# The last projection's first weight tile split after the last expert team's transposes, with two outputs' low weights in the second pass

## The chip, the cores and the metric

The kernel runs on one core of a Trainium2 chip. The metric is the device time of one execution in microseconds (us), the median of several runs. The core has TensorE (PE, the matrix engine, whose weight loads are listed apart as PEld), VectorE (DVE), ScalarE (ACT), GpSimd (POOL), and SyncE (SP), whose queue issues the DMA transfers. SBUF is the working memory of 128 partitions, PSUM the banks into which TensorE accumulates.

## The reference

The program is two model blocks over 256 tokens of width 1024. The first has pooling, sliding-window attention and two dense feed-forward layers; the second has a mixer, then a mixture of experts, then a gated projection, and a last norm. The change touches only the seam between the experts and the gated projection:

```python
h = h + hierarchical_moe(rms_norm_2(h, norm2_g[i]), ...)     # 32 experts, top 2
gate = jax.nn.sigmoid(rms_norm_2(h, ple_norm_g[i]) @ ple_gate_w[i])
h = h + gate * (p[i] @ ple_proj_w[i]).astype(F32)
...
return rms_norm_2(h, final_g).astype(x.dtype)
```

The matrix `ple_gate_w` (1024 x 1024, float32) is called `w_ple` in the kernel; the product with it is "the last projection". It has 8 outputs of 128 columns each, c = 0 to 7, and 8 input chunks of 128, k = 0 to 7.

## The kernel before

**Split weights.** A float32 matrix product is computed from halves of the numbers: each weight w is split into a high part (float32r, a copy by ScalarE in `split_hi`, L707 to L716) and a low part (w minus the high part, by VectorE in `split_lo`, L718 to L726). The same holds for the activations (`xh`, `xl`). A product needs three matmuls: high weights by high activations, low by high, high by low; `mm3` (L1280 to L1286) issues the three. `w_ple` comes as two transfers, each into one ring tile of 2 x 2048 columns. `halves("w_ple", i, PIECE)` names the two half tiles of transfer i, so there are four pieces of 2048 columns, each with two outputs: piece 0 holds outputs 0 and 1, piece 1 outputs 2 and 3, and so on. Piece 0 is split into the buffers `third_h` and `third_l`, piece 1 into `fourth_h` and `fourth_l`, which nothing else uses at this time; pieces 2 and 3 go to `wh` and `wl`. The semaphores `hi_done` and `lo_done` count the split pieces in order; `split_lo` waits on `hi_done` (L721), and `split_hi` of the first half waits for the transfer (L711).

**The experts.** They run as 16 teams of two experts (`for b in range(TEAMS)`, once in each engine's program). On TensorE a team is: `gate_up` (L1672, 32 matmuls), a gather of the tokens of team b + 2 (L1644, L1645; absent for the last two teams), `transposes` (L1678, 2), `combine` of the team before (L1695, 16), `down` (L1686, 16). Between them ScalarE computes `sgate` (Silu, L1140) when `gate_up` is done; VectorE computes `he` from it (L2362); the transposes wait for `he`; ScalarE copies them to `heT` (L1144), for which `down` waits; ScalarE writes `yh` from the output of `down` (L1149, two halves), VectorE writes `yl` (L2370), and `combine` waits for both. In the trace `sgate`, `he` and `heT` bear the name `work`. SP streams the weights of each team into a ring of six chunks (L520); each load waits until the chunk two teams earlier was used. Behind the last chunk it issues the two transfers of `w_ple` (L538).

**The order around the change.** Each engine runs its program strictly in order. In the last team (b = 15) ScalarE's order is: high part of piece 0 (with the wait for its transfer), `sgate`, `heT`, high part of piece 1, `yh`; then the high part of piece 2, then for each of the 8 chunks `xh` (L1153) and a square (L690), then the reciprocal root of the norm (L696, L697), the high part of piece 3, a table load and the sigmoids (L1161). VectorE's order is: low part of piece 0, `he`, low part of piece 1, `yl`; then 8 additions to the residual `hs` (L2380), 8 `xl` (L2384), the low part of piece 2, and per output the scaling by the norm (L2398), the product with the gate and the addition to `hs` (L2393, L2394), with the low part of piece 3 after output 1.

**The last projection on TensorE.** First pass: for each k, as `xh` comes, high and low weights of outputs 0 to 3 by `xh` (64 matmuls, L1792). Then the squares of the norm are summed (L1276). Second pass: for outputs 0 to 3, high weights by `xl` (32 matmuls, L1798), after each output a release `ple_psum`. Then outputs 4 to 7 with `mm3` (24 matmuls each, L1285), with sums of the last norm's squares after each. These squares are computed by GpSimd (L678) as the chunks of `hs` come; GpSimd also adds pairs of the projection norm's squares (L578).

Of the kernel before, what the change touches and what calls it, by code (L numbers as in the profile page):

```python
# [16 lines left out]
KD = D // P  # L17
N_META = 16
SEQ = 256
# [24 lines left out]
TEAMS = NE // TEAM  # L44
# [3 lines left out]
CHUNKS = 3  # L48
# [5 lines left out]
PIECE = 2048  # L54
# [13 lines left out]
FIRST_PIECE = {_name: NUMBER[_name, 0] for _name, _ in SPLIT}  # L68
# [72 lines left out]
def bass_two_blocks(nc, a, out):  # L141
# [4 lines left out]
    with ctx:  # L146
# [5 lines left out]
        def sem(name):  # L152
            if name not in sems:
                sems[name] = ctx.enter_context(nc.semaphore(name))
            return sems[name]
# [37 lines left out]
        with ExitStack() as turn:  # L193
            xh = sb("xh", [P, 9, SEQ], F32R, turn)
            xl = sb("xl", [P, 9, SEQ], F32R, turn)
# [28 lines left out]
        ps = ctx.enter_context(nc.psum_tensor("ps", [P, 8, 512], F32))  # L224
# [149 lines left out]
        for part in SPLIT:  # L374
            if part in THIRD:
                k = 2
            elif part in FOURTH:
                k = 3
            else:
                k, turn_of = turn_of, 1 - turn_of  # L380
# [326 lines left out]
        def split_hi(act, name, slot, rnd, i, j, size):  # L707

            if j == 0:
                act.wait_ge(sem(f"tile_ready{slot}"), loaded(name, slot, rnd))  # L710

            buffer_free(act, name, i, j)
            high, _ = split_buffer(name, i, j)
            for to, src in parts_of(name, high, ring[:, slot, j * size:(j + 1) * size], size):
                ins = act.activation(to, src, ACT.Copy)  # L715
            ins.then_inc(sem("hi_done"), 1)  # L716

        def split_lo(dve, name, slot, rnd, i, j, size):  # L718

            piece = NUMBER[name, i * 2 + j] if type(i) is int else i * 2 + (FIRST_PIECE[name] + j)  # L720
            dve.wait_ge(sem("hi_done"), piece + 1)  # L721
            high, low = split_buffer(name, i, j)
            w = ring[:, slot, j * size:(j + 1) * size]
            for (to, src), (h, _) in zip(parts_of(name, low, w, size), parts_of(name, high, w, size)):
                ins = dve.tensor_tensor(to, src, h.bitcast(F32), ALU.subtract)  # L725
            ins.then_inc(sem("lo_done"), 1)  # L726
# [13 lines left out]
        PLE_BANK = (4, 5, 7, 0, 1, 2, 3, 4)  # L740
# [4 lines left out]
        def halves(name, i, size):  # L745
            slot, rnd = tile_at(FIRST[name] + i)
            return [(slot, rnd, i, j, size) for j in range(2)]
# [105 lines left out]
        def _(act):  # L853
# [279 lines left out]
            act.wait_ge(sem("route_ready"), 1)  # L1133
            for b in range(TEAMS):
                extra(b)
                if b == TEAMS - 1:
                    act.wait_ge(sem("chunk_used"), b * CHUNKS)
                    split_hi(act, "w_ple", *halves("w_ple", 0, PIECE)[0])
                act.wait_ge(sem("chunk_used"), b * CHUNKS + GU_CHUNKS)
                act.activation(sgate, ps[:, 4, 0:FE], ACT.Silu).then_inc(sem("sg_ready"), 1)  # L1140
                if b + 2 < TEAMS:
                    gathered(b + 2)
                act.wait_ge(sem("het_psum"), b + 1)
                act.activation(heT.rearrange("p c n -> p (c n)"), ps[:, 4, 0:FE], ACT.Copy).then_inc(sem("heT_ready"), 1)  # L1144
                if b == TEAMS - 1:
                    split_hi(act, "w_ple", *halves("w_ple", 0, PIECE)[1])
                act.wait_ge(sem("chunk_used"), (b + 1) * CHUNKS)
                for i in range(2):
                    act.activation(yh[:, i * 512:(i + 1) * 512], ps[:, 6 + i, :], ACT.Copy).then_inc(sem("y_ready"), 1)  # L1149
# [106 lines left out]
        def _(pe):  # L1256
            mm = pe.matmul
# [41 lines left out]
            for c in range(KD):  # L1299
# [4 lines left out]
                for k in range(2):  # L1304
                    ins = mm(ps[:, c % 4, 0:T], pw[:, g, k, c % 2 * P:c % 2 * P + P], pooled[:, 2 * g + k, :],
                             start=(k == 0), stop=(k == 1))
# [473 lines left out]
            def ple_weights(c, k):  # L1780
                at = slice(k * 256 + c % 2 * P, k * 256 + c % 2 * P + P)
                return [x[:, at] for x in split_buffer("w_ple", c // 4, c // 2 % 2)]

            for k in range(KD):
                pe.wait_ge(sem("xh_ready"), 4 * KD + k + 1)
                for c in range(4):
                    if k == 0 and c % 2 == 0:
                        pe.wait_ge(sem("lo_done"), FIRST_PIECE["w_ple"] + c // 2 + 1)
                    if k == 0 and c == 3:
                        pe.wait_ge(sem("hs_odd"), 5 * (KD // 2) + 1)  # L1790
                    for part, w in enumerate(ple_weights(c, k)):
                        mm(ps[:, PLE_BANK[c], 0:SEQ], w, xh[:, k, 0:SEQ], start=(k == 0 and part == 0), stop=False)  # L1792
            for q in range(KD):
                sum_squares("ple", q, SEQ)
            for c in range(4):
                for k in range(KD):
                    pe.wait_ge(sem("x_ready"), 4 * KD + k + 1)
                    ins = mm(ps[:, PLE_BANK[c], 0:SEQ], ple_weights(c, k)[0], xl[:, k, 0:SEQ], start=False, stop=(k == KD - 1))  # L1798
                ins.then_inc(sem("ple_psum"), 1)
            for c in range(4, KD):  # L1800
                pe.wait_ge(sem("lo_done"), FIRST_PIECE["w_ple"] + c // 2 + 1)
# [185 lines left out]
        def _(dve):  # L1987
# [368 lines left out]
            placed(0)  # L2356
            for b in range(TEAMS):
                extra(b)
                if b == TEAMS - 1:
                    split_lo(dve, "w_ple", *halves("w_ple", 0, PIECE)[0])  # L2360
                dve.wait_ge(sem("sg_ready"), b + 1)
                dve.scalar_tensor_tensor(he, ps[:, 4, FE:2 * FE], small[:, 178:179], sgate, ALU.mult, ALU.mult)\  # L2362
                   .then_inc(sem("he_ready"), 1)
                if b + 2 < TEAMS:
                    gathered(b + 2)
                if b == TEAMS - 1:
                    split_lo(dve, "w_ple", *halves("w_ple", 0, PIECE)[1])
                for i in range(2):
                    dve.wait_ge(sem("y_ready"), 2 * b + i + 1)
                    dve.tensor_tensor(yl[:, i * 512:(i + 1) * 512], ps[:, 6 + i, :], yh[:, i * 512:(i + 1) * 512].bitcast(F32),  # L2370
                                      ALU.subtract).then_inc(sem("y_low"), 1)
                if b + 1 < TEAMS:
                    dve.wait_ge(sem("he_ready"), b + 1)
                    placed(b + 1)
                if b % 2 and b + 3 < TEAMS:
                    selected(b // 2 + 2)
# [5 lines left out]
            for c in range(KD):  # L2382
                dve.wait_ge(sem("xh_ready"), 4 * KD + c + 1)
                dve.scalar_tensor_tensor(xl[:, c, :], hs[:, c, N_META:], V("ple", c), xh[:, c, :].bitcast(F32),  # L2384
                                         ALU.mult, ALU.subtract).then_inc(sem("x_ready"), 1)
            split_lo(dve, "w_ple", *halves("w_ple", 1, PIECE)[0])
            dve.wait_ge(sem("r_ready"), NORM["ple"] + 1)
            dve.wait_ge(sem("pp_ready"), KD)
# [162 lines left out]
```

## Time and profile before

| | |
|---|---|
| device time, 3 runs | 1058.27 us median (1054.91 to 1059.91) |
| the profiled execution | 1055.95 us, its span 1054.2 us |
| TensorE busy | 975.9 us (93%) |
| VectorE busy | 540.5 us (51%) |
| ScalarE busy | 414.4 us (39%) |
| GpSimd busy | 146.2 us (14%) |
| granted TensorE clock, mean | 0.962 of full speed |

The two experts' lines L1672 and L1686 and the last projection stand in the last quarter of the span: the experts end at about 1011 us, the projection and the last norm fill the rest. Times in the views are microseconds from the start of the span. A row of a timeline gives start, busy time, engine, line, operation and operands, and in brackets how long the engine sat idle before it and what released it. The granted clock (PEclk) has two levels here, 1.00 (2.4 GHz) and 0.50 (1.2 GHz); a value between them is a mean over a stretch with both.

### The profile page before, as it was taken

To read this page: it belongs to the slowest core of one execution; us is meant where nothing else is said; L and a number is where in the kernel's file an instruction comes from. 1 tells how busy PE (TensorE), PEld (TensorE's weight loads), DVE (VectorE), ACT (ScalarE), POOL (GpSimd) and SP (SyncE) were. 2 spreads that over 40 slices of the span, in tenths; PEclk is the share of its full clock that TensorE was granted. 3 is DMA by queue.
4 is the path that set the end of the run, shared out by engine and by line. 5 is a ranking of instruction groups with operands and counts; after the bars stand their busy time and mean duration, and the time that the engine had idled before them with its cause. 6 is when DMAs were issued, how large, how long until landed. Compare 5 with 4: busy or idle time off the path is not lost.

```text
span 1054.2 us, 16922 instructions
## 1 busy us (share of the span) xinstructions
PE 975.9 (93%) x6840; PEld 813.6 (77%) x6840; DVE 540.5 (51%) x1002; ACT 414.4 (39%) x690; POOL 146.2 (14%) x207
## 2 busy tenths in 40 slices
PE   4699999999989999999998999879889999999796
PEld 2599999998868899999987999659745555455285
DVE  4654554437874655554445548574623344333355
ACT  4443334437565634334444457633211111111152
POOL 5323233110000233322000000000100000000002
PEclk7899999999989999999999999769899999999989
DMA  7325553468721345534552512028369999999801
GB/s 294 149 91 180 197 195 109 166 192 214 184 81 35 127 170 200 188 109 172 198 200 87 203 76 85 7 84 330 160 229 417 420 421 418 419 419 420 355 1 40
DMA packets 36798, 212.01 MB, mean 201 GB/s; under 512 B 2528, under 2 KB 16112, under 8 KB 17520
## 3 DMA queue, kind: packets, MB, share of 16 engines
q1 hardware_dynamic: 36720, 210.91, 53.1%
q8 instruction: 56, 0.92, 0.4%
q14 instruction: 22, 0.18, 0.1%
HBM read 209.83 MB, written 1.07 MB: 200 GB/s over the span
## 4 chain that ended last, share of the span: by engine, by line
PE 81%; DVE 9%; ACT 3%; DMA 2%; issue 2%; POOL 2%; POOLq 0%; DVEq 0%; ACTq 0%
PE ps L1285 48%; PE ps L1672 9%; PE ps L1686 5%; PE ps L1695 3%; PE ps L1276 3%; DMA ring<-in_w_ple 2%; PE ps L1209 2%; PE ps L1644 2%; PE ps L1645 1%; DVE mix L1819 1%; DVE wl L725 1%; DVE third_l L725 1%; PE ps L1792 1%; DVE hs L571 1%; PE ps L1217 1%
## 5 line engine op out<-in xcount | busy, mean ns | idle before, releaser
L725 DVE TENSOR_TENSOR wl<-ring,wh 128x2048 fp32r<-128x2048 f32 (+3 forms) x104 | 205.2, 1976 | 189.4 <-ACT wh L715 189.4
L715 ACT ACTIVATE wh<-ring 128x2048 fp32r<-128x2048 f32 (+3 forms) x104 | 172.4, 1660 | 266.7 <-PE ps L1285 264.8
L1285 PE MATMUL ps<-xh,wh 128*128 128x256 f32 (+3 forms) x600 | 171.2, 285 | 0.0
L1285 PE MATMUL ps<-xl,wh 128*128 128x256 f32 (+3 forms) x600 | 169.4, 282 | 0.0
L1285 PE MATMUL ps<-xh,wl 128*128 128x256 f32 (+3 forms) x600 | 169.4, 282 | 0.0
L1285 PEld LDWEIGHTS ps<-xh,wh 128*128 128x128 f32 (+3 forms) x600 | 111.0, 185 | 1.2 <-issue 0.9
L1285 PEld LDWEIGHTS ps<-xh,wl 128*128 128x128 f32 (+3 forms) x600 | 111.0, 185 | 0.2
L1285 PEld LDWEIGHTS ps<-xl,wh 128*128 128x128 f32 (+3 forms) x600 | 110.9, 185 | 0.0
L1285 PE MATMUL ps<-acth,wh 128*128 128x272 f32 (+1 forms) x352 | 101.1, 287 | 0.0
L1285 PE MATMUL ps<-actl,wh 128*128 128x272 f32 (+1 forms) x352 | 100.0, 284 | 0.0
L1285 PE MATMUL ps<-acth,wl 128*128 128x272 f32 (+1 forms) x352 | 100.0, 284 | 0.0
L1285 PE MATMUL ps<-xhT,wl 128*128 128x272 f32 x320 | 92.6, 289 | 0.0
L1285 PE MATMUL ps<-xlT,wh 128*128 128x272 f32 x320 | 92.2, 288 | 0.0
L1285 PE MATMUL ps<-xhT,wh 128*128 128x272 f32 x320 | 91.3, 285 | 0.0
L1285 PEld LDWEIGHTS ps<-acth,wh 128*128 128x128 f32 x352 | 66.5, 189 | 0.2
L1285 PEld LDWEIGHTS ps<-acth,wl 128*128 128x128 f32 x352 | 66.1, 188 | 0.2
L1285 PEld LDWEIGHTS ps<-actl,wh 128*128 128x128 f32 x352 | 66.2, 188 | 0.0
L2370 DVE TENSOR_TENSOR yl<-ps,yh 128x512 fp32r<-128x512 f32 x32 | 20.6, 685 | 87.6 <-ACT yh L1149 87.6
L1285 PEld LDWEIGHTS ps<-xhT,wh 128*128 128x128 f32 x320 | 60.4, 189 | 0.0
L1285 PEld LDWEIGHTS ps<-xlT,wh 128*128 128x128 f32 x320 | 60.1, 188 | 0.0
L1285 PEld LDWEIGHTS ps<-xhT,wl 128*128 128x128 f32 x320 | 60.1, 188 | 0.0
L1686 PE MATMUL ps<-wring,work 128*64 128x512 f32 x256 | 58.5, 598 | 0.6 <-ACT work L1144 0.6
(418 smaller groups left out, 1853.1 us busy)
## 6 DMA issues: line engine op xcount, KB each, us to landing
wring<-in_w_eg SPq DMA_DIRECT2D x32, 2048.0 KB, 15.0
ring<-in_w_gu SPq DMA_DIRECT2D x22, 2048.0 KB, 8.1
wring<-in_w_ed SPq DMA_DIRECT2D x16, 2048.0 KB, 13.5
ring<-in_w_dn SPq DMA_DIRECT2D x16, 1408.0 KB, 5.9
ring<-in_w_z SPq DMA_DIRECT2D x7, 2048.0 KB, 7.8
ring<-in_w_out SPq DMA_DIRECT2D x4, 1152.0 KB, 5.1
ring<-in_w_q SPq DMA_DIRECT2D x8, 512.0 KB, 6.3
ring<-in_w_o SPq DMA_DIRECT2D x8, 512.0 KB, 17.0
```

The costliest lines, as they stand in the source:

```text
L571: eng.tensor_tensor(hs[:, c, cols], hs[:, c, cols], mix[:, c, 0:n], ALU.add).then_inc(hs_add(c), 1)
L715: ins = act.activation(to, src, ACT.Copy)
L725: ins = dve.tensor_tensor(to, src, h.bitcast(F32), ALU.subtract)
L1209: pe.matmul(ps[:, 2 * j + g, 0:n], w[:, k * 256 + g * P:k * 256 + g * P + P], xa[:, k, 0:n], start=(k == 0 and part == 0), stop=False)
L1217: ins = pe.matmul(ps[:, 2 * j + g, 0:n], w[:, k * 256 + g * P:k * 256 + g * P + P], xb[:, k, 0:n], start=False, stop=(k == KD - 1))
L1276: mm(ps[:, 6, 0:n], ones[0:rows, :], square_at(name, c + 1 - chunks)[0:rows, 0:n], start=(c < chunks), stop=(c == last))\
L1285: ins = mm(o, p, q, start=first and n == 0, stop=last and n == 2)
L1644: mm(out, h2h[:, k, at], select[:, k, :], start=(k == 0), stop=False)
L1672: ins = mm(ps[rows, 4, :], x[:, k, rows], chunk(b, c)[:, j, i * 512:(i + 1) * 512], start=(k == 0), stop=(k == KD - 1))
L1686: ins = mm(ps[rows, 6 + i, :], heT[:, k, rows], chunk(b, GU_CHUNKS)[:, j, k * D + i * 512:k * D + (i + 1) * 512], start=(k == 0), stop=(k ...
L1695: ins = mm(ps[:, c // 2, c % 2 * SEQ:(c % 2 + 1) * SEQ], y[:, c * P:(c + 1) * P], weights, start=False, stop=last and y is parts[-1], skip ...
L2370: dve.tensor_tensor(yl[:, i * 512:(i + 1) * 512], ps[:, 6 + i, :], yh[:, i * 512:(i + 1) * 512].bitcast(F32), ALU.subtract).then_inc(sem(" ...
```

## The change

In the last team, ScalarE no longer makes the high part of piece 0 ahead of `sgate`: it makes those of pieces 0 and 1 one after the other, behind `heT` and ahead of `yh`. VectorE makes the low part of piece 0 behind `he` (where that of piece 1 was), and that of piece 1 behind the eight `xl`, ahead of the low part of piece 2. On TensorE the first pass uses both parts of the weights for outputs 0 and 1 but the high part alone for outputs 2 and 3 (48 matmuls); their 16 matmuls of low weights by `xh` go to the second pass. The waits change with them: for the low part of piece 0 and the high part of piece 1 ahead of the first pass, for the low part of piece 1 ahead of output 2 of the second pass. No transfer moves and no operation is added or taken away.

```diff
--- before.py
+++ after.py
@@ -1133,9 +1133,6 @@
             act.wait_ge(sem("route_ready"), 1)
             for b in range(TEAMS):
                 extra(b)
-                if b == TEAMS - 1:
-                    act.wait_ge(sem("chunk_used"), b * CHUNKS)
-                    split_hi(act, "w_ple", *halves("w_ple", 0, PIECE)[0])
                 act.wait_ge(sem("chunk_used"), b * CHUNKS + GU_CHUNKS)
                 act.activation(sgate, ps[:, 4, 0:FE], ACT.Silu).then_inc(sem("sg_ready"), 1)
                 if b + 2 < TEAMS:
@@ -1143,7 +1140,8 @@
                 act.wait_ge(sem("het_psum"), b + 1)
                 act.activation(heT.rearrange("p c n -> p (c n)"), ps[:, 4, 0:FE], ACT.Copy).then_inc(sem("heT_ready"), 1)
                 if b == TEAMS - 1:
-                    split_hi(act, "w_ple", *halves("w_ple", 0, PIECE)[1])
+                    for x in halves("w_ple", 0, PIECE):
+                        split_hi(act, "w_ple", *x)
                 act.wait_ge(sem("chunk_used"), (b + 1) * CHUNKS)
                 for i in range(2):
                     act.activation(yh[:, i * 512:(i + 1) * 512], ps[:, 6 + i, :], ACT.Copy).then_inc(sem("y_ready"), 1)
@@ -1781,21 +1779,26 @@
                 at = slice(k * 256 + c % 2 * P, k * 256 + c % 2 * P + P)
                 return [x[:, at] for x in split_buffer("w_ple", c // 4, c // 2 % 2)]
 
+            pe.wait_ge(sem("lo_done"), FIRST_PIECE["w_ple"] + 1)
+            pe.wait_ge(sem("hi_done"), FIRST_PIECE["w_ple"] + 2)
             for k in range(KD):
                 pe.wait_ge(sem("xh_ready"), 4 * KD + k + 1)
                 for c in range(4):
-                    if k == 0 and c % 2 == 0:
-                        pe.wait_ge(sem("lo_done"), FIRST_PIECE["w_ple"] + c // 2 + 1)
                     if k == 0 and c == 3:
                         pe.wait_ge(sem("hs_odd"), 5 * (KD // 2) + 1)
-                    for part, w in enumerate(ple_weights(c, k)):
+                    for part, w in enumerate(ple_weights(c, k)[0:2 - c // 2]):
                         mm(ps[:, PLE_BANK[c], 0:SEQ], w, xh[:, k, 0:SEQ], start=(k == 0 and part == 0), stop=False)
             for q in range(KD):
                 sum_squares("ple", q, SEQ)
             for c in range(4):
+                if c == 2:
+                    pe.wait_ge(sem("lo_done"), FIRST_PIECE["w_ple"] + 2)
                 for k in range(KD):
                     pe.wait_ge(sem("x_ready"), 4 * KD + k + 1)
-                    ins = mm(ps[:, PLE_BANK[c], 0:SEQ], ple_weights(c, k)[0], xl[:, k, 0:SEQ], start=False, stop=(k == KD - 1))
+                    high, low = ple_weights(c, k)
+                    if c >= 2:
+                        mm(ps[:, PLE_BANK[c], 0:SEQ], low, xh[:, k, 0:SEQ], start=False, stop=False)
+                    ins = mm(ps[:, PLE_BANK[c], 0:SEQ], high, xl[:, k, 0:SEQ], start=False, stop=(k == KD - 1))
                 ins.then_inc(sem("ple_psum"), 1)
             for c in range(4, KD):
                 pe.wait_ge(sem("lo_done"), FIRST_PIECE["w_ple"] + c // 2 + 1)
@@ -2356,15 +2359,13 @@
             placed(0)
             for b in range(TEAMS):
                 extra(b)
-                if b == TEAMS - 1:
-                    split_lo(dve, "w_ple", *halves("w_ple", 0, PIECE)[0])
                 dve.wait_ge(sem("sg_ready"), b + 1)
                 dve.scalar_tensor_tensor(he, ps[:, 4, FE:2 * FE], small[:, 178:179], sgate, ALU.mult, ALU.mult)\
                    .then_inc(sem("he_ready"), 1)
                 if b + 2 < TEAMS:
                     gathered(b + 2)
                 if b == TEAMS - 1:
-                    split_lo(dve, "w_ple", *halves("w_ple", 0, PIECE)[1])
+                    split_lo(dve, "w_ple", *halves("w_ple", 0, PIECE)[0])
                 for i in range(2):
                     dve.wait_ge(sem("y_ready"), 2 * b + i + 1)
                     dve.tensor_tensor(yl[:, i * 512:(i + 1) * 512], ps[:, 6 + i, :], yh[:, i * 512:(i + 1) * 512].bitcast(F32),
@@ -2383,6 +2384,7 @@
                 dve.wait_ge(sem("xh_ready"), 4 * KD + c + 1)
                 dve.scalar_tensor_tensor(xl[:, c, :], hs[:, c, N_META:], V("ple", c), xh[:, c, :].bitcast(F32),
                                          ALU.mult, ALU.subtract).then_inc(sem("x_ready"), 1)
+            split_lo(dve, "w_ple", *halves("w_ple", 0, PIECE)[1])
             split_lo(dve, "w_ple", *halves("w_ple", 1, PIECE)[0])
             dve.wait_ge(sem("r_ready"), NORM["ple"] + 1)
             dve.wait_ge(sem("pp_ready"), KD)
```

## Rows read from the trace of the kernel before

**Rows 1.** Chain of work that ended last: start us, us, what ran.
```profile
969.32 1.91 PE ps L1695 x16
...
978.29 18.37 DMA ring<-in_w_ple
...
996.73 1.92 ACT third_h L715
...
998.74 2.29 DVE third_l L725
```

**Rows 2.** Timeline of TensorE: start, busy us, instruction, idle before and its releaser.
```profile
974.64 7.04 PE L1672 MATMUL ps<-wring,work 128*64 128x512 f32 x32
982.75 0.44 PE L1678 MATMUL ps<-cst,work 128*128 128x128 f32 x2 [1.07 <-DVE work L2362]
...
985.02 3.65 PE L1686 MATMUL ps<-wring,work 128*64 128x512 f32 x16
988.50 7.04 PE L1672 MATMUL ps<-wring,work 128*64 128x512 f32 x32
1001.48 0.69 PE L1678 MATMUL ps<-cst,work 128*128 128x128 f32 x2 [5.94 <-DVE work L2362]
...
1003.04 0.41 PE L1695 MATMUL ps<-places,yl 128*128 128x256 f32 x1
1003.25 0.41 PE L1695 MATMUL ps<-places,yh 128*128 128x256 f32 x1
...
1005.31 3.65 PE L1686 MATMUL ps<-wring,work 128*64 128x512 f32 x16
1011.03 0.36 PE L1695 MATMUL ps<-places,yh 128*128 128x256 f32 x1 [2.06 <-ACT yh L1149]
```

**Rows 3.** Timeline of ScalarE (ACT), same columns.
```profile
981.73 0.38 ACT L1140 ACTIVATE work<-ps 128x256 f32<-128x256 f32 x1 [5.78 <-PE ps L1672]
983.22 0.39 ACT L1144 ACTIVATE work<-ps 128x256 f32<-128x256 f32 x1 [1.11 <-PE ps L1678]
...
1017.60 0.40 ACT L690 ACTIVATE mix<-hs 128x256 f32<-128x256 f32 x1
...
1025.20 1.90 ACT L715 ACTIVATE wh<-ring 128x2048 fp32r<-128x2048 f32 x1
```

**Rows 4.** Timeline of VectorE (DVE), same columns.
```profile
982.21 0.48 DVE L2362 SCALAR_TENSOR_TENSOR work<-ps,small,work 128x256 f32<-128x256 f32 x1 [2.19 <-ACT work L1140]
...
1014.85 4.30 DVE L2384 SCALAR_TENSOR_TENSOR xl<-hs,vec,xh 128x256 fp32r<-128x256 f32 x8
1019.07 2.28 DVE L725 TENSOR_TENSOR wl<-ring,wh 128x2048 fp32r<-128x2048 f32 x1
1025.51 0.42 DVE L2398 TENSOR_TENSOR mix<-ps,rstd 128x256 f32<-128x256 f32 x1 [4.16 <-PE ps L1798]
```

**Rows 5.** Stretches: length; PE, PEld, DVE, ACT, POOL busy; PEclk, DMA share, GB/s.
```profile
1001.50:1003.50 2.00, 2.00 (x10) 2.00 (x11) 0.00 (x0) 1.29 (x2) 0.00 (x0) 0.50 0.03 8
1011.70:1015.00 3.30, 3.30 (x18) 3.30 (x17) 3.02 (x9) 2.96 (x9) 0.74 (x1) 0.52 0.00 0
```

**Rows 6.** Timeline of TensorE, last projection.
```profile
1022.11 2.32 PE L1276 MATMUL ps<-mix,ones 128*128 128x256 f32 x10
1024.08 2.25 PE L1798 MATMUL ps<-xl,third_h 128*128 128x256 f32 x16
...
1030.79 0.28 PE L1285 MATMUL ps<-xl,wh 128*128 128x256 f32 x1
1032.57 0.67 PE L1276 MATMUL ps<-sq,ones 128*128 128x256 f32 x2 [1.50 <-POOL sq L678]
```

**Rows 7.** Timeline of GpSimd (POOL), squares of the last two norms.
```profile
1016.66 1.01 POOL L578 TENSOR_TENSOR mix<-mix 128x256 f32<-128x256 f32 x1 [0.66 <-ACT mix L690]
1029.83 2.59 POOL L678 TENSOR_TENSOR sq<-hs 128x256 f32<-128x256 f32 x1 [12.16 <-DVE hs L2394]
1033.24 0.61 POOL L678 TENSOR_TENSOR sq<-hs 128x256 f32<-128x256 f32 x1 [0.82 <-DVE hs L2394]
```

## Prediction

> **What bounds the kernel now.** I read the page first: TensorE is busy 93% of the span, so only its idle time and its time at the lower clock are to be had. Then the chain of waits near the end, where the change is. In it the reader should see that TensorE's chain is broken behind the last team's `gate_up`: a transfer of `w_ple`, issued at 978.29 us, takes 18.37 us, and behind it stand the high part of piece 0 (1.92), and its low part (2.29) [rows 1]; `he` (0.48) [rows 4] follows on the same engine. So the last team's transposes wait for a weight that they don't need, only because ScalarE and VectorE work in program order.
>
> The timeline of TensorE gives the size. Team 14 is the model of an undisturbed last team, since neither it nor team 15 gathers: its `gate_up` ends at 974.64 + 7.04 = 981.68 and its transposes start at 982.75, 1.07 us later. Team 15's `gate_up` ends at 988.50 + 7.04 = 995.54, and its transposes start at 1001.48 behind 5.94 us of idleness [rows 2]. The rest of the sum is read from the views behind that: the clock by stretch, the last projection on TensorE, and the other engines' timelines.
>
> **The change, part by part.** Everything up to 995.54 stays, the transfers included: SP waits for the same `chunk_used` counts, which team 14 gives.
>
> *Step 1, the stall.* `sgate` now starts when `gate_up` is done, as in team 14 (981.73), and `he` at once behind it (982.21) [rows 3, 4]. The transposes start at 995.54 + 1.07 = 996.61 in place of 1001.48: **4.87 us** won.
>
> *Step 2, the clock.* Behind the 5.94 us the granted clock is 0.50 [rows 5], the 1.2 GHz level. There the matmuls of `combine` follow one another at 1003.25 - 1003.04 = 0.21 us [rows 2]; at full clock the same 16 took 1.91 us [rows 1], 0.119 each. Team 14's 1.07 us of idleness was followed by no such fall: from its transposes to the end of `down` are 985.02 + 3.65 - 982.75 = 5.92 us, against 1005.31 + 3.65 - 1001.48 = 7.48 in team 15 [rows 2]. I take 5.92: **1.56 us** won, `down` ends at 1002.53 in place of 1008.96. The bounds are 0 (the fall comes anyway) and 1.56.
>
> *Step 3, the copies ahead of `yh`.* `heT` starts 0.47 us behind the transposes and lasts 0.39 [rows 2, 3], so it ends at 997.47. The transfer landed by 996.73 [rows 1] and is no longer waited for. The two high parts, some 1.9 us each [rows 1, 3], end at about 1001.3; `yh` is due at 1002.5. This cover is 1.2 us: `yh` waits only if the transfer lands after about 998.7, and then us for us. VectorE's low part of piece 0 (2.29) runs from 999.4 to 1001.7, and `yl` is due at about 1003.2. So both cost nothing, and the idleness behind `down` stays at the 2.06 us shown [rows 2]: `combine` starts at 1011.03 - 6.43 = 1004.60. Queued behind the two copies on ScalarE are `yh`, the high part of piece 2 and the eight `xh`; all move up by the same 6.43.
>
> *Step 4, the first pass.* It loses 16 matmuls of 1.91 / 16 = 0.119 us [rows 1], so 1.91 us, and the norm's sums start at 1022.11 - 6.43 - 1.91 = 1013.77. What would be late instead: `xh` and the squares. The last square ended at 1018.00 [rows 3], GpSimd's last pair sum at 1017.67 [rows 7]; with the 6.43 both are at about 1011.5, so they don't hold TensorE. The new waits ahead of the pass (low part of piece 0, high part of piece 1) were met by 1001.7. Cost nothing.
>
> *Step 5, the second pass.* It gains the same 16 matmuls, so TensorE's total work is unchanged, and from output 4 on the shift is 6.43 again. It starts at 1024.08 - 8.34 = 1015.74 and comes to output 2 behind 16 matmuls, at about 1017.7. VectorE ends `xl` at 1019.15 - 6.43 = 1012.7, and then makes the low part of piece 1 (2.3) until 1015.0 and that of piece 2 (2.3) until 1017.3 [rows 4]. The first is due at 1017.7 (cover 2.7), the second at output 4, about 1021.6. Behind them on VectorE is the scaling of output 0, which was due at 1025.51 - 8.34 = 1017.17 [rows 4], when VectorE is just free. Should it be late by the whole 2.28 us, ScalarE's high part of piece 3 (1.90) and a table load stand ahead of the first sigmoid and hide most of it.
>
> *Step 6, the idle time after output 4.* Output 4 ended at 1030.79 + 0.28 = 1031.07 and TensorE then sat 1.50 us for GpSimd's first square of `hs` [rows 6], 2.59 us long, where the next took 0.61 [rows 7]. That square hangs on the norm, which comes 8.34 us earlier (step 4), while output 4 comes only 6.43 earlier. It is done at 1032.42 - 8.34 = 1024.08, against 1031.07 - 6.43 = 1024.64: the **1.50 us** go, with 0.56 us to spare. Bounds 0 and 1.50. From there TensorE's work binds, output by output, to the end as before.
>
> The long square ran while VectorE made the low part of piece 3. The Trainium skill (SBUF — State Buffer, on the shared port pair) says that a GpSimd operation that reads SBUF and a VectorE one with two SBUF inputs lock each other out for a whole instruction. The trace agrees with its 2.59 beside 0.61. It speaks against moving a low part, of that very kind, to a place where GpSimd works; here GpSimd's pair sums are over by then, and by the rule the sum stays the same.
>
> *The sum:* 4.87 + 1.56 + 1.50 = **7.93 us**. Against the profiled execution's own time that is 1055.95 - 7.93 = 1048.0. The median of the runs shown is 2.3 us above that execution: 1058.27 - 7.93 = 1050.3. If what made the other runs longer is a later transfer, the new kernel doesn't feel it (step 3); if it is something else, it does. I take the middle, 1049.2.
>
> **The rivals.**
> *A: the second fall of the clock goes too.* Behind the 2.06 us of idleness the clock was 0.52 from 1011.7 to 1015.0 [rows 5]. From 1011.03 to 1022.11 lie 16 + 64 matmuls, 11.08 us, against 80 x 0.119 = 9.55: the fall costs 1.53. It followed a stretch that had already been slow once; with TensorE fuller ahead of it, it may stay away. Against: the idle time is as long as before. Gain 9.46, time 1047.7 by the same middle. The Trainium skill (TensorE: Matmul & The Clock Gate, Part 1) says that where the transition falls varies from run to run of one kernel. That leaves both cases open.
>
> *B: a cover fails.* GpSimd's 0.56 us is the thinnest: a second lock-out, or VectorE late at 1017.2, brings back up to 1.50. Or the clock falls already behind the 1.07 us (1.56 back). Gain 4.87 to 6.4, time about 1051.5.
>
> *C: the stall isn't there in most runs.* It depends on 1.1 us between `gate_up`'s end and the landing. If transfers ran ahead by 3 us or more in the other runs, piece 0's parts would be nearly done by 995.5 and only steps 4 to 6 would count: gain 1.5 to 3, time about 1056. Against: the other runs are mostly longer, not shorter, than the profiled one.
>
> *D: slower.* The clock falls behind the 2.06 us and stays at 1.2 GHz, since TensorE's work now meets more waits. A matmul of the projection then costs 0.21 in place of 0.119 [rows 1, 2]. The gain is eaten after 7.93 / 0.091 = 87 more such matmuls; if the level stayed down through the projection, about 190 matmuls beyond those already slow, it would cost 17 and end at about 1066. Against: both falls shown ended while TensorE was working.
>
> **How the numbers follow.** Forecast (7.93) 0.50, A 0.22, B 0.17, C 0.08, D 0.03. The range holds the forecast, A and B over the spread of the runs shown: from 1054.91 - 9.46 = 1045.5 to 1059.91 - 6.43 = 1053.5. A difference under 0.5% (5.3 us) is about what a measurement of this kernel can't tell from no change. Faster by more: forecast, A and two thirds of B, 0.84; within: the rest of B and C, 0.13; slower: D, 0.03.
>
> **What would show it.** Step 1: `sgate` starts 0.05 us behind `gate_up`, and the idle time before the last transposes is about 1.1 us, with no transfer in the chain. Step 2: the last `combine` but one takes 1.9 us. Step 3: ScalarE is idle before `yh`, and TensorE's idleness before the last `combine` is still 2.06. Step 5: no idle time before output 2 of the second pass. Step 6: none after output 4. The prediction is wrong if `yh` waits behind the copies, if the clock is low for longer than the one stretch of 3.3 us that rows 5 show, or if TensorE waits for GpSimd or VectorE in the last projection.

## The result

The changed kernel takes 1048.05 us (median of 5 runs, 1046.90 to 1050.14) against 1058.22 for the kernel before in the same comparison (1054.18 to 1059.91). The ratio is 0.9915, with a 95% interval of 0.9896 to 0.9933: some 9 us less, between 7 and 11. The profiled execution took 1047.29 us, its span 1045.5.

Spans of two executions differ by what happened hundreds of microseconds earlier, too. So from here on one measure is used for all traces, **M: the time from the end of the last team's `gate_up` to the end of the span**, since all that the change touches lies in it. Before, M is 1054.2 - 995.54 = 58.66 us [rows 2]; after, 1045.5 - 996.46 = 49.04. That is 9.62 less, while the spans differ by 8.7: `gate_up` ended 0.92 later in the execution of after.

The chain of waits of the changed kernel around the last transposes (start us, us, what ran; in the new file `gate_up` is L1670, `sgate` L1137, `he` L2363, `transposes` L1676):

```profile
989.59 6.89 PE ps L1670 x32
...
996.50 0.39 ACT work L1137
...
996.99 0.49 DVE work L2363
...
997.53 0.44 PE ps L1676 x2
...
1003.51 0.03 ACT yh L1147
```

The reader should see what is gone against [rows 1]: no transfer and no split stands between `gate_up` and the transposes, only `sgate` and `he`. The timeline of TensorE gives the sizes:

```profile
989.42 7.04 PE L1670 MATMUL ps<-wring,work 128*64 128x512 f32 x32
997.53 0.44 PE L1676 MATMUL ps<-cst,work 128*128 128x128 f32 x2 [1.07 <-DVE work L2363]
...
999.81 3.65 PE L1684 MATMUL ps<-wring,work 128*64 128x512 f32 x16
1005.53 0.36 PE L1693 MATMUL ps<-places,yh 128*128 128x256 f32 x1 [2.07 <-ACT yh L1147]
```

The idle time before the last transposes is 1.07 us in place of 5.94 [rows 2]; from the transposes to the end of `down` are 999.81 + 3.65 - 997.53 = 5.93 us in place of 7.48. The idle time before the last `combine` is unchanged, 2.07. ScalarE and VectorE of the changed kernel, to be held against [rows 3, 4]:

```profile
996.50 0.38 ACT L1137 ACTIVATE work<-ps 128x256 f32<-128x256 f32 x1 [5.78 <-PE ps L1670]
...
998.28 1.90 ACT L715 ACTIVATE third_h<-ring 128x2048 fp32r<-128x2048 f32 x1
1000.08 1.90 ACT L715 ACTIVATE fourth_h<-ring 128x2048 fp32r<-128x2048 f32 x1
1003.51 1.08 ACT L1147 ACTIVATE yh<-ps 128x512 fp32r<-128x512 f32 x2 [1.53 <-PE ps L1684]
```

```profile
1000.22 2.29 DVE L725 TENSOR_TENSOR third_l<-ring,third_h 128x2048 fp32r<-128x2048 f32 x1 [2.75 <-ACT third_h L715]
...
1008.94 4.24 DVE L2385 SCALAR_TENSOR_TENSOR xl<-hs,vec,xh 128x256 fp32r<-128x256 f32 x8
1013.09 2.28 DVE L725 TENSOR_TENSOR fourth_l<-ring,fourth_h 128x2048 fp32r<-128x2048 f32 x1
1015.29 2.28 DVE L725 TENSOR_TENSOR wl<-ring,wh 128x2048 fp32r<-128x2048 f32 x1
1017.50 0.74 DVE L2400 TENSOR_TENSOR mix<-ps,rstd 128x256 f32<-128x256 f32 x2
```

Both high parts end at 1001.98, and ScalarE then sits idle for 1.53 us before `yh`: the copies are hidden. The low part of piece 1 (`fourth_l`) ends at 1015.37, and output 2 of the second pass starts on TensorE at 1017.26, with no idle time before it. The scaling of output 0 starts at 1017.50, right when the low part of piece 2 is done. TensorE around the sums of the norm and after output 4, and GpSimd's squares, which answer to [rows 6, 7]:

```profile
1013.21 2.32 PE L1274 MATMUL ps<-mix,ones 128*128 128x256 f32 x10
1015.18 2.25 PE L1801 MATMUL ps<-xl,third_h 128*128 128x256 f32 x16
...
1023.79 0.28 PE L1283 MATMUL ps<-xl,wh 128*128 128x256 f32 x1
1023.91 0.59 PE L1274 MATMUL ps<-sq,ones 128*128 128x256 f32 x2
```

```profile
1020.94 2.59 POOL L678 TENSOR_TENSOR sq<-hs 128x256 f32<-128x256 f32 x1 [8.84 <-DVE hs L2396]
1024.35 0.62 POOL L678 TENSOR_TENSOR sq<-hs 128x256 f32<-128x256 f32 x1 [0.82 <-DVE hs L2396]
```

No idle time stands in front of the sum at 1023.91, where [rows 6] have 1.50. GpSimd's first square is still 2.59 us long, but it ends at 1023.53, 0.54 us ahead of output 4 (1023.79 + 0.28).

The clock by stretch (length; busy time of PE, PEld, DVE, ACT, POOL; granted clock, DMA share, GB/s):

```profile
996.50:1002.00 5.50, 4.47 (x28) 2.92 (x30) 2.27 (x2) 4.36 (x4) 0.00 (x0) 1.00 0.29 118
1005.50:1008.00 2.50, 2.47 (x21) 2.50 (x22) 1.72 (x6) 2.16 (x5) 0.00 (x0) 1.00 0.00 0
```

The granted clock is 1.00 (2.4 GHz) in both stretches where [rows 5] show 0.50 and 0.52. So neither fall came here, and the forecast had the second one.

### The profile page after: what moved, and what is told of

Read it like the earlier page. It is cut to its first block, busy times and chain, and to the rows that moved or that the text cites. A ratio compares the mean times of both kernels' runs of the same rounds, so it can differ in the third digit from the quotient of the medians.

```text
span 1045.5 us, 16918 instructions
## 1 busy us (share of the span) xinstructions
PE 973.9 (93%) x6835; PEld 809.7 (77%) x6840; DVE 540.0 (52%) x1002; ACT 414.2 (40%) x690; POOL 146.6 (14%) x207
## 3 DMA queue, kind: packets, MB, share of 16 engines
HBM read 209.83 MB, written 1.07 MB: 202 GB/s over the span
## 4 chain that ended last, share of the span: by engine, by line
PE 83%; DVE 9%; ACT 3%; issue 2%; POOL 2%; DMA 0%; POOLq 0%; DVEq 0%; ACTq 0%
PE ps L1283 48%; PE ps L1670 11%; PE ps L1684 5%; PE ps L1693 3%; PE ps L1274 3%; PE ps L1642 2%; PE ps L1207 2%; PE ps L1643 2%; DVE mix L1822 1%; DVE wl L725 1%; PE ps L1215 1%; DVE hs L571 1%; PE ps L1628 1%; DVE third_l L725 1%; PE ps L1790 1%
## 5 line engine op out<-in xcount | busy, mean ns | idle before, releaser
L1670 PE MATMUL ps<-wring,xb_even 128*64 128x512 f32 x256 | 58.5, 607 | 2.2 <-issue 2.2
```

The source lines that it names most:

```text
L1670: ins = mm(ps[rows, 4, :], x[:, k, rows], chunk(b, c)[:, j, i * 512:(i + 1) * 512], start=(k == 0), stop=(k == KD - 1))
```

## The experiments

All measures in one place. "Idle 1" and "idle 2" are TensorE's idle times before the last transposes and before the last `combine`; T is the time from these transposes to the end of `down`; "sq" is the idle time after output 4. A fall is a stretch at 0.50. The traces of e3, i1 and i2 stand with those runs.

| kernel | M | idle 1 | T | idle 2 | sq | fall behind idle 1 | behind idle 2 |
|---|---|---|---|---|---|---|---|
| before | 58.66 | 5.94 | 7.48 | 2.06 | 1.50 | yes | yes |
| after | 49.04 | 1.07 | 5.93 | 2.07 | 0 | no | no |
| after, once more | 50.60 | 1.07 | 5.93 | 2.07 | 0 | no | yes |
| e1, splits only | 52.63 | 1.07 | 5.93 | 2.55 | 1.43 | no | yes |
| e2, second pass only | 56.67 | 6.20 | 8.37 | 2.07 | 0 | yes | no |
| e4, before, low part 3 later | 57.37 | 6.14 | 8.36 | 2.07 | 0 (0.56 later) | yes | no |
| e5, before, transfer late | 58.21 | 5.99 | 8.43 | 2.07 | 1.49 | yes | no |
| e6, after, transfer late | 49.08 | 1.08 | 5.92 | 2.07 | 0 | no | no |
| e7, before, transfer later | 61.64 | 9.43 | 8.44 | 2.07 | 1.49 | yes | no |
| e8, after, transfer later | 51.87 | 1.07 | 5.93 | 3.17 | 0 | no | yes |
| e9, before, stall filled | 55.32 | 5.64, filled | 5.94 | 2.07 | 1.49 | no | no |

**Each part alone (e1, e2).** The first experiment keeps TensorE's program and moves only the splits; both low parts are then ahead of `yl`. The second undoes just that move in the changed kernel.

```diff
 e1, against before; ScalarE (VectorE likewise, with split_lo, behind he):
-                if b == TEAMS - 1:
-                    act.wait_ge(sem("chunk_used"), b * CHUNKS)
-                    split_hi(act, "w_ple", *halves("w_ple", 0, PIECE)[0])
...
                 if b == TEAMS - 1:
-                    split_hi(act, "w_ple", *halves("w_ple", 0, PIECE)[1])
+                    for x in halves("w_ple", 0, PIECE):
+                        split_hi(act, "w_ple", *x)
 e2, against after: high and low part of piece 0 again ahead of sgate and he
```

> Before, with the splits of pieces 0 and 1 moved behind heT on ScalarE and behind he on VectorE, both low parts still ahead of yl, TensorE's program untouched. Measure: from the end of the last team's gate_up to the end of the span, 58.7 us in the kernel before, 49.0 after. Theory (the stall and its clock carry the gain, 4.87 + 1.56): idle time before the last transposes 1.1 us; yl about 0.6 us later, since VectorE now makes two low parts ahead of it; the 1.5 us before GpSimd's square stay. That gives 52.8, or 51.3 if the second fall of the clock is gone too. Rival (the second pass carries the gain): above 57.

> After, with piece 0 split ahead of sgate and he again, as before; the low weights of outputs 2 and 3 stay in the second pass. Theory: the 5.94 us of idleness before the last transposes stay, the wait for GpSimd's first square after output 4 goes: 58.7 - 1.5 = 57.2 us from the end of gate_up to the end. Rival (the second pass carries the gain): 53 or less.

e1 measured 52.63 us, against 52.8 expected with a fall; its ratio to the kernel before is 0.9929 (0.9905 to 0.9953). e2 measured 56.67 against 57.2; its ratio is 0.9992 (0.9980 to 1.0005). By these ratios the moved splits carry 7.5 of some 9 us, and the second pass alone can't be told from no change; the traces give it the 1.5 us of the column sq and little more. In e1's timelines the second pass's own use is to be seen (TensorE, then VectorE):

```profile
997.34 0.44 PE L1676 MATMUL ps<-cst,work 128*128 128x128 f32 x2 [1.07 <-DVE work L2358]
...
1005.82 0.55 PE L1693 MATMUL ps<-places,yh 128*128 128x256 f32 x1 [2.55 <-issue]
```

```profile
1000.03 2.29 DVE L725 TENSOR_TENSOR third_l<-ring,third_h 128x2048 fp32r<-128x2048 f32 x1 [2.75 <-ACT third_h L715]
1002.24 2.29 DVE L725 TENSOR_TENSOR fourth_l<-ring,fourth_h 128x2048 fp32r<-128x2048 f32 x1
1004.44 1.28 DVE L2367 TENSOR_TENSOR yl<-ps,yh 128x512 fp32r<-128x512 f32 x2
```

The low part of piece 1 stands between `third_l` and `yl` there, so `yl` starts at 1004.44, and idle 2 is 2.55 in place of 2.07. Moving 16 matmuls into the second pass lets that low part go behind `xl`: it is worth 0.5 us there, and lets the 1.43 us before GpSimd's square go. The rest of the 3.59 us between e1 and the changed kernel is the fall behind the 2.55 us.

**The transfer moved (e5 to e8).** The same one-line edit to the kernel before and to the changed one; the wait of SP ahead of the first transfer of `w_ple`:

```diff
-            for i, count in ((0, (TEAMS - 2) * CHUNKS + 1), (1, (TEAMS - 1) * CHUNKS)):
+            for i, count in ((0, (TEAMS - 1) * CHUNKS), (1, (TEAMS - 1) * CHUNKS)):           # e5, e6
+            for i, count in ((0, (TEAMS - 1) * CHUNKS + 1), (1, (TEAMS - 1) * CHUNKS + 1)):   # e7, e8
```

> Before, with the first transfer of w_ple issued only when team 14 has used its last chunk (some 10 us later, together with the second). Theory: the stall is the landing of this transfer, so the idle time before the last transposes grows from 5.9 us by as much as the transfer lands later, about 2 to 4 us, and the time from gate_up to the end grows by the same, 60.7 to 62.7. Rival (the stall is the two splits alone): 58.7.

> After, with the same late transfer. Theory (step 3's cover): the idle time before the last transposes stays at 1.07; yh waits for the two high parts only by what the landing is later than 2.2 us behind the end of gate_up. Landing 3 us behind: both high parts end at 6.8 and yh, due at 7.05, doesn't wait, 49.0 us. Landing 5 us behind: yh waits 1.8 us, about 50.9 us and perhaps a fall of the clock (1.5 more). Rival (the change only moves the wait): as much longer as the kernel before becomes.

These two missed their aim. In e5 the transfer was issued 10 us later and landed 1.24 us behind `gate_up`, where the earlier one of the kernel before had landed 1.19 us behind: issued behind a full queue it had taken 18.4 us [rows 1], and issued behind a shorter one 8.0. The DMA rates bear this out: in the kernel before, the core's DMA engines moved 410 GB/s over those 18.4 us (978.29 to 996.66), some 7.5 MB, of which this transfer is 2.1; in e5 they moved 353 GB/s over the 8.0 (991 to 999), some 2.8 MB. Both sums are estimates, rate times time. Nothing moved that could be tested. (They serve as a second trace of each kernel instead.) So the issue was put later still:

> Before, with both transfers of w_ple issued only when the last team has used its first chunk, 3.5 us before the end of its gate_up. In the late run before this one a transfer issued 6.8 us before that end landed 8.0 us later; with 8 us again it lands 4.5 us behind gate_up's end in place of 1.2. Theory (the stall is this landing plus the two splits): idle time before the last transposes 9.3 us in place of 5.9, 61.5 to 62 us from gate_up to the end.

> After, with the same issue of the transfers. Theory (step 3): idle time before the last transposes still 1.07; the first high part starts at the landing, 4.5 us behind gate_up, both end at 8.3, and yh, due at 7.05, is 1.3 us late; 50.3 us from gate_up to the end in place of 49.0, and up to 1.5 more if the clock falls behind the longer idle time. Rival (the change only moves the wait): 3.3 us longer, like the kernel before.

In e7 the landing is at 1004.14, 4.68 us behind `gate_up` (999.46), 3.44 later than in e5. ScalarE's row, then TensorE's:

```profile
1004.14 1.91 ACT L715 ACTIVATE third_h<-ring 128x2048 fp32r<-128x2048 f32 x1 [10.41 <-DMA ring<-in_w_ple]
```

```profile
1008.89 0.69 PE L1678 MATMUL ps<-cst,work 128*128 128x128 f32 x2 [9.43 <-DVE work L2362]
```

Idle 1 grew by 3.44 us and M by 3.43, one for one. The ratio to the kernel before is 1.0034 (1.0018 to 1.0049), so the runs show it too. In e8, the changed kernel with a landing 4.55 us behind `gate_up` (998.13), first ScalarE, then TensorE:

```profile
1002.68 1.91 ACT L715 ACTIVATE third_h<-ring 128x2048 fp32r<-128x2048 f32 x1 [2.63 <-DMA ring<-in_w_ple]
1004.50 1.89 ACT L715 ACTIVATE fourth_h<-ring 128x2048 fp32r<-128x2048 f32 x1
1006.30 1.06 ACT L1147 ACTIVATE yh<-ps 128x512 fp32r<-128x512 f32 x2
```

```profile
999.20 0.44 PE L1676 MATMUL ps<-cst,work 128*128 128x128 f32 x2 [1.07 <-DVE work L2363]
...
1008.30 0.36 PE L1693 MATMUL ps<-places,yh 128*128 128x256 f32 x1 [3.17 <-ACT yh L1147]
```

The last transposes don't notice the transfer (1.07). `yh` stands right behind the second copy, and idle 2 is 3.17, 1.10 more than 2.07. M is 2.83 more than 49.04: 1.10 for the wait, and 1.73 with a fall of the clock behind it. The expectation had 1.3 and up to 1.5. So the cover of step 3 is real and has an edge: `yh` waits once the transfer lands more than 4.55 - 1.10 = 3.45 us behind `gate_up`. The prediction's own terms put it at 3.2 (998.7 - 995.54); the "2.2 us" in the expectation of e6 is a slip, since its own cases (3 us: no wait, 5 us: 1.8) follow from 3.2. The ratio of e8 to the kernel before is 0.9923 (0.9903 to 0.9943): with this late transfer too the changed kernel is the faster one.

**The clock by itself (e9).** The stall of the kernel before is kept, but TensorE is given work on nothing in it:

```diff
+                if b == TEAMS - 1:
+                    stay_busy(pe, 5, 25)
                 pe.wait_ge(sem("he_ready"), b + 1)
```

> Before, with 25 bf16 matmuls on nothing (0.213 us each, 5.3 us) in the idle time ahead of the last transposes: the stall stays, the clock shouldn't fall. Theory (step 2: the clock is 1.56 us of the gain by itself): no stretch at 0.5 behind the stall, from the transposes to the end of down 5.9 us in place of 7.5, and 57.1 us from gate_up to the end, 55.6 if no fall comes behind the idle time after down either. Rival (the clock costs nothing of its own there): 58.7. Idle time as filled is counted as idle.

```profile
995.41 5.57 PE L1183 MATMUL ps<-cst 128*128 128x512 bf16 x25
1001.12 0.44 PE L1678 MATMUL ps<-cst,work 128*128 128x128 f32 x2
...
1003.41 3.65 PE L1686 MATMUL ps<-wring,work 128*64 128x512 f32 x16
```

T is 1003.41 + 3.65 - 1001.12 = 5.94 us, as in the changed kernel, and M is 55.32 against 55.6 expected for the case without a second fall. The stall itself is 1001.12 - 995.48 = 5.64 us, ended by `he` as before. Against e5, which has no second fall either, M is 2.89 less: 2.49 in T and 0.35 by the shorter stall. The ratio to the kernel before is 0.9968 (0.9949 to 0.9988), 1.3 to 5.4 us less. The stall's clock is a cost of its own, and mostly more than the 1.56 us of the prediction: in e2, e4, e5 and e7 the low clock reached into `down`, and T was 8.36 to 8.44, 2.4 to 2.5 us above 5.93 (in e3 it was 8.22).

Why the size differs can be read from the clock by stretch. First the kernel before, whose transposes start at 1001.48, then e5, whose transposes start at 1003.78:

```profile
1004.50:1005.00 0.50, 0.50 (x5) 0.50 (x4) 0.50 (x1) 0.00 (x0) 0.00 (x0) 0.52 0.00 0
1005.00:1005.50 0.50, 0.50 (x5) 0.36 (x6) 0.50 (x1) 0.00 (x0) 0.00 (x0) 1.00 0.00 0
```

```profile
1009.00:1009.50 0.50, 0.50 (x4) 0.03 (x2) 0.01 (x1) 0.00 (x0) 0.00 (x0) 0.65 0.00 0
1009.50:1010.00 0.50, 0.50 (x6) 0.21 (x4) 0.00 (x0) 0.00 (x0) 0.00 (x0) 1.00 0.00 0
```

A mean of 0.65 over half a microsecond is 0.35 us at 0.50 and the rest at 1.00. So the clock is back at full speed 3.5 us behind the transposes in the kernel before, and 5.6 us behind them in e5 (5.4 in e2 and e4, 5.6 in e7, 5.2 in e3). In each of these traces T is longer than 5.93 by 0.44 or 0.45 of that time. So what the stall's clock costs depends on how much of TensorE's work falls under the low clock, and the profiled execution of the kernel before had less of it than any other trace with an unfilled stall.

**The second fall (e3, i1, and the changed kernel once more).** Matmuls on nothing were put between the last `down` and the last `combine` of the kernel before (e3) and of the changed one (i1):

```diff
+            stay_busy(pe, 5, 18)
             pe.wait_ge(sem("y_ready"), 2 * TEAMS)
```

> Before, with 18 bf16 matmuls on nothing (about 1.9 us) in the idle time between the last down and the last combine. Theory A (the second fall of the clock comes from this idle time and costs 1.53): no stretch at 0.5 behind it, 57.1 us from gate_up to the end. Rival (the fall comes whatever is done there, or by chance): 58.7 and a slow stretch somewhere in the projection. If the filling delays combine, it is longer than 58.7.

> After, with the same 18 matmuls. If the fall of the clock behind the 2.07 us is gone in the kernel after in every execution, nothing changes: 49.0 us from gate_up to the end and the median of after. If it comes in some executions (rival: chance), the median is up to 1 us under that of after and the spread is narrower.

The filling was mis-sized: the 18 matmuls of `stay_busy`, of 512 columns each, take 3.83 us, 0.213 each, not the 0.106 to which "about 1.9 us" comes. The row of i1 (it counts 17 of the 18) shows it running past the moment when `combine` could have started:

```profile
1005.50 3.83 PE L1181 MATMUL ps<-cst 128*128 128x512 bf16 x17 [0.16 <-issue]
```

M rose to 60.33 in e3, 2.12 above e5, and to 50.76 in i1, 1.72 above the changed kernel. The runs can't tell e3 from the kernel before (1.0010, 0.9986 to 1.0034), and the ratio of i1 is 0.9916 (0.9883 to 0.9949). No fall came behind it in either, but none came in most unfilled traces, so these two don't decide between the theories. The repeat of the changed kernel does:

> The changed kernel once more, for the clock behind the 2.07 us before the last combine. If its absence belongs to the change: no fall, 49.0 us from gate_up to the end. If it is chance: a fall in some executions, then 50.5.

```profile
987.06 7.04 PE L1670 MATMUL ps<-wring,work 128*64 128x512 f32 x32
995.16 0.44 PE L1676 MATMUL ps<-cst,work 128*128 128x128 f32 x2 [1.07 <-DVE work L2363]
...
997.44 3.65 PE L1684 MATMUL ps<-wring,work 128*64 128x512 f32 x16
1003.16 0.36 PE L1693 MATMUL ps<-places,yh 128*128 128x256 f32 x1 [2.07 <-ACT yh L1147]
```

```profile
1003.00:1006.70 3.70, 3.54 (x18) 3.57 (x19) 2.32 (x8) 3.13 (x7) 0.51 (x1) 0.56 0.00 0
```

The same kernel with the same idle times had the fall this time (0.56 from 1003.0 to 1006.7), and M is 1044.7 - 994.10 = 50.60, 1.56 more than 49.04. So its absence does not belong to the change. Behind an idle time of 2.06 or 2.07 us it came in 2 of 9 traces (before, and the changed kernel once more), and it costs 1.5 us when it does. Rival A's price was right. What decides whether the fall comes is not shown: it came once with the stall ahead and once without, and stayed away five times with it (once filled, e9) and twice without.

**GpSimd's long square (e4).** In the kernel before, the low part of piece 3 is made behind output 2 (`if c == 2`) in place of output 1.

> Before, with VectorE's low part of piece 3 one output later (after output 2 of the loop in place of output 1). Theory (GpSimd's first square of hs is long, 2.59 us, because VectorE makes that low part at the same time): the first square takes 0.6 us and the 1.50 us of TensorE's idleness after output 4 go; the second square, which now meets the low part, takes 2 us or more, and TensorE waits some 0.7 us for the third. From the end of gate_up to the end 57.9 us in place of 58.7. Rival (the first square is long because GpSimd has sat idle long): the first square stays at 2.6 us and the 1.5 us stay.

GpSimd's squares in e4, and VectorE's low part of piece 3:

```profile
1034.40 0.61 POOL L678 TENSOR_TENSOR sq<-hs 128x256 f32<-128x256 f32 x1 [10.75 <-DVE hs L2394]
1035.84 2.59 POOL L678 TENSOR_TENSOR sq<-hs 128x256 f32<-128x256 f32 x1 [0.82 <-DVE hs L2394]
1039.25 0.61 POOL L678 TENSOR_TENSOR sq<-hs 128x256 f32<-128x256 f32 x1 [0.82 <-DVE hs L2394]
```

```profile
1035.67 2.28 DVE L725 TENSOR_TENSOR wl<-ring,wh 128x2048 fp32r<-128x2048 f32 x1
```

The first square, behind 10.75 us of idleness, takes 0.61 us; the second, started 0.17 us behind the low part, takes 2.59 and ends at 1038.43, 0.48 us behind the end of the low part (1037.95). So the length comes from the low part and not from idleness. TensorE's 1.50 us after output 4 are gone, and 0.56 come back at the next sum; M is 57.37 against 58.21 in e5, a trace with the same falls. The runs can't tell it (0.9995, 0.9975 to 1.0015). The Trainium skill's rule (SBUF — State Buffer, on the shared port pair) is borne out: which of GpSimd's operations waits goes with where the low part is put.

**A shorter last combine (i2).** `combine` needs only the first halves of `yh` and `yl` for its first four outputs:

```diff
+                    if last and c % 4 == 0:
+                        pe.wait_ge(sem("y_ready"), 2 * TEAMS - 1 + c // 4)
+                        pe.wait_ge(sem("y_low"), 2 * TEAMS - 1 + c // 4)
...
-            pe.wait_ge(sem("y_ready"), 2 * TEAMS)
-            pe.wait_ge(sem("y_low"), 2 * TEAMS)
```

> After, with the last combine waiting for the first halves of yh and yl ahead of its first four outputs and for the second halves ahead of the other four. The idle time before it was 2.07 us, of which the second halves are 0.5 (yh) and 0.6 (yl): expected 1.4 us, 0.6 us less, and from gate_up to the end 48.4 us. If VectorE's additions to hs bind behind it, less than that. The median then is 0.6 us under that of after, which the runs can't tell; the trace can.

```profile
1008.80 0.36 PE L1696 MATMUL ps<-places,yh 128*128 128x256 f32 x1 [1.52 <-DVE yl L2372]
```

Idle 2 is 1.52 us in place of 2.07 (1.4 expected), and M 48.62 in place of 49.04 (48.4 expected). It is the shortest M of all; its median of 1048.00 us and ratio of 0.9902 (0.9876 to 0.9928) can't be told from those of the changed kernel.

## Why the prediction was right, and where it was off

The prediction was 1049.2 us, and 1048.05 was measured. Point by point:

- **Step 1, the stall (4.87):** right. Idle 1 went from 5.94 to 1.07. e7 shows that the landing sets it one for one, e8 that in the changed order the transposes don't feel it.
- **Step 2, the clock (1.56):** the mechanism was right (e9), the size was read from one execution, the one with the least work under the low clock. In the five other traces with an unfilled stall T is 8.22 to 8.44 and the term 2.3 to 2.5.
- **Step 3, the copies ahead of `yh` (0):** right. ScalarE had 1.53 us to spare, against a cover put at 1.2; with the landing past the edge `yh` waited, 1.10 us in e8.
- **Steps 4 and 5 (0):** right. `fourth_l` was ready 1.9 us before output 2 needed it, a cover put at 2.7; TensorE came earlier, for want of a second fall.
- **Step 6 (1.50):** right, with 0.54 us to spare against 0.56 forecast; e2 has it alone and e1 lacks it.
- **The second fall:** the sum kept it, since the one trace had it and the idle time stayed. It is the less usual case. Without it the profiled pair gives 4.87 + 1.56 + 1.53 + 1.50 = 9.46 of the 9.62 measured, which is rival A. Of the 0.16 left over the table says where they lie: M less the two idle times, T and sq is 39.97 to 40.03 us in the traces with the new second pass and no second fall (after, e2, e6), and 40.18 to 40.24 in those with the old one (e4, e5, e7, e9; for e4 its 0.56 taken off). So some 0.2 us go with the second pass; why is open.
- **The base of the sum:** the middle between the profiled execution's own time and the median was the wrong choice. `gate_up` of the last team ends between 994.10 and 1000.53 us in the 14 traces, whose programs are the same up to there but for the issue of the transfers of `w_ple` in four of them; the median is 997.86, 2.3 later than in the profiled execution of before. So most executions are longer ahead of the change, by something that the change doesn't touch, and the median was the base to use. From 1058.27 the sum with usual sizes (5.0 + 2.45 + 1.5, and no second fall on either side) gives 1049.3.

So two errors cancel in the predicted time: a base 1.16 us too low, and a gain some 1.0 us too small. That 1049.2 and 1049.3 agree is luck. The gain with usual sizes, 8.95 us, is what the ratio gives (9.0, between 7 and 11); the medians themselves differ by 10.2, and that 1.2 us more is within this interval.

Rival C (no stall in most runs) is refuted by the landing. It asked for transfers 3 us or more earlier. In the ten traces whose transfer was not moved, the landing lay from 1.6 us behind the end of `gate_up` (e3) to 0.2 ahead of it: i1 alone has it ahead, with 981.07 + 17.1 = 998.2 against 998.34, and even there two splits would have stood between `gate_up` and `he` in the old order. The rival's "about 1056" is also a slip: a gain of 1.5 to 3 from the middle base of 1057.1 is 1054.1 to 1055.6. Rivals B and D didn't come.

## What to carry to other kernels

An engine that works in program order should not meet the wait for a transfer ahead of a short operation for which TensorE waits. Put the long copies behind it, and check how late the transfer may then be before the next short operation waits. A stall of TensorE costs its length and, where the clock falls in it, the work done at the lower clock behind it (here 5 us, and 1.6 to 2.5 more), so the gain of removing one can be more than the idle time. A term that hangs on the clock is to be sized from more than one execution, and the base for a predicted median is the median.

## What the runs showed of the hardware

- Behind the same 2.06 to 2.07 us of TensorE's idleness the granted clock fell to 0.50 in 2 of 9 traces, once with and once without the stall ahead; behind the 1.07 us before the last transposes it did in none of 7, in the stalls of 5.94 us and more in all 6. Behind 1.52 us it stayed up in the one trace, behind 2.55 and 3.17 us it fell in the one trace of each. The Trainium skill (TensorE: Matmul & The Clock Gate, Part 1) says that the place of a transition varies from run to run of one kernel. Here that goes as far as whether a fall comes at all: two traces of the changed kernel differ by 1.56 us for it.
- A 2 MB transfer took 18.4 us from issue to landing behind a full queue and 8.0 us when issued some 10 us later, and landed at the same distance from the end of `gate_up` (1.19 and 1.24 us). That delay cost nothing (e5: 1.0003, 0.9982 to 1.0024). Issued 3.4 us later still (e7) it again took some 8 us, and landed 3.44 us later.
- A GpSimd square of 128x256 took 2.59 us in place of 0.61 when it started 0.17 us behind a VectorE low part of 2.28 us, and the long one was another square when the low part was moved (e4).
